# Rotary and plain halves of two attention heads handled as a pair in a two-layer hybrid encoder kernel

## What is computed

```python
q = (rms_norm(c_q, mla_q_norm_g[l]) @ mla_w_uq[l]).reshape(B, S, MLA_HEADS, MLA_QK)
kv = (rms_norm(c_kv, mla_kv_norm_g[l]) @ mla_w_ukv[l]).reshape(B, S, MLA_HEADS, MLA_NOPE + MLA_V)
k_nope, v_m = kv[..., :MLA_NOPE], kv[..., MLA_NOPE:]
k = jnp.concatenate([k_nope, jnp.broadcast_to(k_rope[:, :, None, :], ...)], axis=-1)
q, k = rms_norm(q, mla_qn_g[l]), rms_norm(k, mla_kn_g[l])
q = jnp.concatenate([q[..., :MLA_NOPE], rope(q[..., MLA_NOPE:], pos)], axis=-1)
k = jnp.concatenate([k[..., :MLA_NOPE], rope(k[..., MLA_NOPE:], pos)], axis=-1)
...
s = jnp.einsum('bqhd,bkhd->bhqk', q[:, q0:q1], k[:, :q1]).astype(jnp.float32) * scale
mask = (jnp.arange(q1) // CHUNK)[None, :] <= ((q0 + jnp.arange(Q_BLOCK)) // CHUNK)[:, None]
p = jax.nn.softmax(jnp.where(mask, s, -jnp.inf), axis=-1)
```

## Time and profile before

| | |
|---|---|
| profiled execution / its span | 1735.35 / 1733.6 us |
| median of the runs | 1735.27 us |
| PE busy | 1714.8 us, 8730 matmul records |
| DVE, ACT, POOL busy | 1104.6, 862.1, 296.0 us |
| granted TensorE clock | 0.999 of full speed |
| PE idle, named waits | 5.9 (first x), 4.3 (w_lo), 3.3 (L1518), 0.6 (L1442) us |

### The profile page before, as it was taken

One profiled execution on the slowest core, in us unless ns is written; L12 is line 12 of the kernel. 1 busy time (PEld: TensorE's weight loads), 2 busy tenths in 40 slices (PEclk: granted clock), 3 DMA queues, 4 the chain that ended last, 5 costly groups with the idle time before them and its releaser, 6 DMA issues.

```text
span 1733.6 us, 22527 instructions
## 1 busy us (share of the span) xinstructions
PE 1714.8 (99%) x8730; PEld 1435.9 (83%) x8730; DVE 1104.6 (64%) x1571; ACT 862.1 (50%) x1267; POOL 296.0 (17%) x440
## 2 busy tenths in 40 slices
PE   7999999999999999999999999999999999999998
PEld 6878888888888888888888788888888888888887
DVE  4667564656766647786656775755666666668853
ACT  6454543434455555555454445434445555655532
POOL 1011020210000025362410110110100000444500
PEclk9999999999999999999999999999999999999999
DMA  8866555655655556795687655656465555568764
GB/s 258 252 184 181 170 164 177 183 152 176 195 165 150 166 174 200 229 310 197 200 260 225 182 175 161 183 158 183 147 193 176 169 156 158 163 215 273 273 197 153
DMA packets 177475, 332.84 MB, mean 192 GB/s; under 512 B 20588, under 2 KB 33306, under 8 KB 177368
## 3 DMA queue, kind: packets, MB, share of 16 engines
q1 hardware_dynamic: 167784, 297.67, 56.0%
q0 software_dynamic: 9584, 33.73, 5.8%
HBM read 311.18 MB, written 16.78 MB: 189 GB/s over the span
## 4 chain that ended last, share of the span: by engine, by line
PE 93%; DVE 2%; ACT 1%; DMA 1%; POOL 1%; issue 1%; SPq 0%; DVEq 0%; ACTq 0%; POOLq 0%
PE D L652 82%; PE B L652 9%; DMA ring<-in_w_in 1%; DVE w_lo L1313 1%; POOL arena L591 1%; ACT w_hi L954 0%; DVE xy L1313 0%; ACT arena L954 0%; PE B L724 0%; PE B L826 0%; DVE arena L1436 0%; SPq L492 0%; PE B L708 0%; DMA xy<-in_x 0%; POOL arena L567 0%
## 5 line engine op out<-in xcount | busy, mean ns | idle before, releaser
L1313 DVE TENSOR_TENSOR w_lo<-ring,w_hi 128x1024 fp32r<-128x1024 f32 (+3 forms) x560 | 668.8, 1208 | 385.0 <-ACT w_hi L954 377.2
L954 ACT ACTIVATE w_hi<-ring 128x1024 fp32r<-128x1024 f32 (+3 forms) x560 | 572.6, 1037 | 373.5 <-PE D L652 272.9
L652 PE MATMUL D<-w_hi,ht_hi 128*128 128x512 f32 (+2 forms) x1728 | 689.0, 399 | 4.4 <-DVE w_lo L1313 4.3
L652 PE MATMUL D<-w_hi,ht_lo 128*128 128x512 f32 (+2 forms) x1728 | 667.4, 386 | 0.0
L652 PE MATMUL D<-w_lo,ht_hi 128*128 128x512 f32 (+2 forms) x1728 | 666.5, 386 | 0.0
L652 PEld LDWEIGHTS D<-w_hi,ht_hi 128*128 128x128 f32 x1728 | 326.0, 189 | 67.5 <-issue 5.9
L652 PEld LDWEIGHTS D<-w_hi,ht_lo 128*128 128x128 f32 x1728 | 325.1, 188 | 65.9
L652 PEld LDWEIGHTS D<-w_lo,ht_hi 128*128 128x128 f32 x1728 | 326.2, 189 | 57.9 <-issue 0.5
L954 ACT ACTIVATE arena<-B 64x128 f32<-64x128 f32 (+5 forms) x200 | 72.2, 368 | 246.3 <-PE B L652 212.6
L652 PEld LDWEIGHTS B<-arena 128*66 128x66 f32 (+4 forms) x1536 | 161.7, 164 | 32.4 <-issue 9.8
L591 POOL COPY arena<-arena 32x256 f32<-32x256 f32 x240 | 162.4, 676 | 126.9 <-DVE arena L1341 82.7
(11 more groups left out here) (155 smaller groups left out, 1288.7 us busy)
## 6 DMA issues: line engine op xcount, KB each, us to landing
ring<-in_w_in SPq DMA_DIRECT2D x368, 512.0 KB, 4.2
ring<-in_w_out SPq DMA_DIRECT2D x64, 512.0 KB, 5.0
ring<-in_w_br_mla SPq DMA_DIRECT2D x32, 512.0 KB, 5.2
gate_spill<-gev POOLq DMA_DIRECT2D x24, 512.0 KB, 4.8
arena<-gate_spill POOLq DMA_DIRECT2D x24, 512.0 KB, 6.0
ring<-in_mla_w_ukv SPq DMA_DIRECT2D x16, 512.0 KB, 4.1
...
```

The source lines that it names most:

```text
L652: return nc.tensor.matmul(o, a, b, start=start, stop=stop, skip_group_check=True)
L954: return nc.scalar.activation(o, i, fn, **kw)
L1313: return v.tensor_tensor(o, a, b, op)
```

## The change

For the two heads of a pair at once: PE transposes the plain parts into `B0` and `B1`, and the rotary parts of both heads together, as blocks of 128 columns, into `B2` (`QRH` and `KRH` hold two heads side by side). ACT copies `B0` and `B2`, DVE `B1`. The scores of head 0 go to `B3`, of head 1 to `B2`; their rotary part is a matmul over rows 0 to 63 for one head and over rows 64 to 127 for the other. DVE writes -1e30 into the masked quadrants in the banks with two memsets, takes four maxima; ACT takes four exponentials; the probabilities' transposes, copies (ACT head 0, DVE head 1) and value matmuls follow, and DVE scales with two operations. The gains are multiplied in with the scaling (`scalar_tensor_tensor`), so the two gain multiplications and the copy back before `ml_qk` go; the gain rows are loaded 192 wide. `ML_STEPS` has 7 entries that sum to 13.0 in place of 11 that sum to 15.4, which moves all positions, and the weights of pair 3 (`uq2`, `ukv2`) come after `sk`.

```diff
@@ -128,8 +123,8 @@
     g = [("wk", "w_in", C_KR, 256, KD)]
     g += wide("rr", C_RW) + wide("rk", C_RW + 512) + wide("rv", C_RW + 1024)
     g += gates[:1] + wide("cq", C_CQ) + wide("ckv", C_CKV)
-    g += gates[1:9] + pair(0) + pair(1) + gates[9:11] + wide("sq", C_SB) + pair(2)
-    g += wide("sk", C_SB + 512) + wide("sv", C_SB + 1024) + pair(3)
+    g += gates[1:9] + pair(0) + pair(1) + gates[9:11] + wide("sq", C_SB)
+    g += wide("sk", C_SB + 512) + pair(2) + wide("sv", C_SB + 1024) + pair(3)
     g += [("rg", "w_in", C_RG + 64, 448, KD)] + gates[11:]
     g += wide("mg0", C_MG) + wide("mg1", C_MG + 512) + wide("sg", C_SB + 1536)
...
@@ -159,7 +154,7 @@
 RW_STEPS = [1, 1.3, 1.2] + [0.9, 1] * LEVELS + [1] * 6
 LATENT_STEPS = [2, 2.5]
 GN_STEPS = [1] * 8
-ML_STEPS = [2.2, 2.2, 2.4] + [1, 1.3, 1, 1] * 2
+ML_STEPS = [2.4, 2.6, 1.6, 1.5, 2, 1.5, 1.4]
 SB_STEPS = [1.5, 3, 2, 2]
 RW_BEATS, GN_BEATS, ML_BEATS, SB_BEATS = len(RW_STEPS), len(GN_STEPS), len(ML_STEPS), len(SB_STEPS)
...
@@ -800,43 +795,54 @@
                     last.then_inc(lat_pe[l], 1)
                 beat()
 
-            def mla_head(m):
-
-                b, i = m // 2 % 2, m % 2
-                if i == 0:
-                    pe.wait_ge(ml_qk, 4 * l + m // 2 + 1)
-                if m:
-                    pe.wait_ge(ml_dve, 24 * l + 3 * m)
+            def mla_pair(p):
+
+                b = p % 2
+                pe.wait_ge(ml_qk, 4 * l + p + 1)
+                for i in range(2):
+                    for h in range(HALVES):
+                        nc.tensor.transpose(B[i][:, h * P:(h + 1) * P], MQ[:, b, h, i, 0:NOPE], ident)
+                        last = nc.tensor.transpose(B[i][:, 256 + h * P:256 + (h + 1) * P], MKV[:, b, h, i, 0:NOPE],
+                                                   ident)
+                    last.then_inc(ml_pe, 1)
+                for j, t in enumerate((QRH, KRH)):
+                    for h in range(HALVES):
+                        last = nc.tensor.transpose(B[2][:, j * 256 + h * P:j * 256 + (h + 1) * P],
+                                                   t[:, h, :, :].rearrange("p n c -> p (n c)"), ident)
+                last.then_inc(ml_pe, 1)
+                beat()
+                pe.wait_ge(ml_act, 16 * l + 4 * p + 1)
+                pe.wait_ge(ml_dve, 16 * l + 4 * p + 1)
+                own = [slice(64 * i, 64 * i + 64) for i in range(2)]
                 for h in range(HALVES):
-                    nc.tensor.transpose(B[0][:, h * P:(h + 1) * P], MQ[:, b, h, i, 0:NOPE], ident)
-                    nc.tensor.transpose(B[0][:, 256 + h * P:256 + (h + 1) * P], MKV[:, b, h, i, 0:NOPE], ident)
-                    nc.tensor.transpose(B[1][0:64, h * P:(h + 1) * P], MQ[:, b, h, i, NOPE:QK], ident)
-                    last = nc.tensor.transpose(B[1][0:64, 256 + h * P:256 + (h + 1) * P], KRH[:, h, i, :], ident)
+                    q, k, o = slice(h * P, (h + 1) * P), slice(256, 384 + h * P), slice(h * P, (2 * h + 1) * P)
+                    for i in range(2):
+                        mm(B[3 - i][:, o], QKN[:, i, q], QKN[:, i, k], True, False)
+                    for i in range(2):
+                        last = mm(B[3 - i][:, o], QKR[own[i], q], QKR[own[i], k], False, True)
                 last.then_inc(ml_pe, 1)
                 beat()
-                pe.wait_ge(ml_act, 24 * l + 3 * m + 1)
-                pe.wait_ge(ml_dve, 24 * l + 3 * m + 1)
-                mm(B[2][:, 0:128], QKN[:, 0:128], QKN[:, 256:384], True, False)
-                mm(B[2][:, 0:128], QKR[0:66, 0:128], QKR[0:66, 256:384], False, True)
-                mm(B[2][:, 128:384], QKN[:, 128:256], QKN[:, 256:512], True, False)
-                mm(B[2][:, 128:384], QKR[0:66, 128:256], QKR[0:66, 256:512], False, True).then_inc(ml_pe, 1)
-                beat()
-                pe.wait_ge(ml_act, 24 * l + 3 * m + 2)
-                for n in range(3):
-                    last = nc.tensor.transpose(B[3][:, n * P:(n + 1) * P], PP[:, n * P:(n + 1) * P], ident)
+                for i in range(2):
+                    pe.wait_ge(ml_act, 16 * l + 4 * p + 2 + i)
+                    for n in range(3):
+                        last = nc.tensor.transpose(B[i][:, n * P:(n + 1) * P], PP[:, i, n * P:(n + 1) * P], ident)
+                    last.then_inc(ml_pe, 1)
+                beat()
+                pe.wait_ge(ml_act, 16 * l + 4 * p + 4)
+                pe.wait_ge(ml_dve, 16 * l + 4 * p + 3)
+                for i in range(2):
...
-                    act.wait_ge(ml_dve, 24 * l + 3 * m + 2)
-                    f(PP[:, 0:128], B[2][:, 0:128], ACT.Exp, scale=ML_SCALE, bias=nb[:, 0:1], accum_out=den[:, 0:1])
-                    f(PP[:, 128:384], B[2][:, 128:384], ACT.Exp, scale=ML_SCALE, bias=nb[:, 1:2],
-                      accum_out=den[:, 1:2]).then_inc(ml_act, 1)
-                    beat()
-                    act.wait_ge(ml_pe, 32 * l + 4 * m + 3)
-                    f(PT, B[3][:, 0:384]).then_inc(ml_act, 1)
-                    beat()
-                    beat()
+                act.wait_ge(ml_pe, 28 * l + 7 * p + 1)
+                f(QKN[:, 0, :], B[0][:])
+                act.wait_ge(ml_pe, 28 * l + 7 * p + 3)
+                f(QKR, B[2][:]).then_inc(ml_act, 1)
+                beat()
+                act.wait_ge(ml_dve, 16 * l + 4 * p + 2)
+                for i in range(2):
+                    f(PP[:, i, 0:128], B[3 - i][:, 0:128], ACT.Exp, scale=ML_SCALE, bias=nb[:, i:i + 1],
+                      accum_out=den[:, i:i + 1])
+                    f(PP[:, i, 128:384], B[3 - i][:, 128:384], ACT.Exp, scale=ML_SCALE, bias=nb[:, 2 + i:3 + i],
+                      accum_out=den[:, 2 + i:3 + i]).then_inc(ml_act, 1)
+                beat()
+                act.wait_ge(ml_pe, 28 * l + 7 * p + 5)
+                f(PT[:, 0, :], B[0][:, 0:384]).then_inc(ml_act, 1)
+                beat()
+                beat()
 
...
                     for i in range(2):
                         k = 2 * h + i
-                        v.tensor_scalar(mq[:, h, i, :], mq[:, h, i, :], qss[:, k:k + 1], None, ALU.mult)
+                        v.scalar_tensor_tensor(mq[:, h, i, :], mq[:, h, i, :], qss[:, k:k + 1], GR[:, 0:QK],
+                                               ALU.mult, ALU.mult)
                         v.tensor_scalar(mk[:, h, i, 0:NOPE], mk[:, h, i, 0:NOPE], nss[:, k:k + 1], None, ALU.mult)
                         last = v.tensor_scalar(KRH[:, h, i, :], KR[:, h, :], nss[:, k:k + 1], None, ALU.mult)
                 link(last)
                 beat()
+                rope(mq[:, :, :, NOPE:QK], QRH, QS[:, 256:512], 2)
+                dve.sem_inc(ml_qk, 1)
+                beat()
+                dve.wait_ge(ml_pe, 28 * l + 7 * p + 2)
+                v.tensor_copy(QKN[:, 1, :], B[1][:]).then_inc(ml_dve, 1)
+                beat()
+                dve.wait_ge(ml_pe, 28 * l + 7 * p + 4)
+                for i in range(2):
+                    last = v.memset(B[3 - i][0:64, :].rearrange("p (n c) -> p n c", n=2)[:, :, 64:128], MASKED)
+                link(last)
+                for i in range(2):
+                    v.reduce_max(mx[:, i:i + 1], B[3 - i][:, 0:128], axis=X)
+                    last = v.reduce_max(mx[:, 2 + i:3 + i], B[3 - i][:, 128:384], axis=X)
+                link(last)
+                v.tensor_scalar(nb, mx, -ML_SCALE, None, ALU.mult).then_inc(ml_dve, 1)
+                beat()
+                dve.wait_ge(ml_act, 16 * l + 4 * p + 3)
+                link(v.reciprocal(rden, den))
+                dve.wait_ge(ml_pe, 28 * l + 7 * p + 6)
+                v.tensor_copy(PT[:, 1, :], B[1][:, 0:384]).then_inc(ml_dve, 1)
+                beat()
+                dve.wait_ge(ml_pe, 28 * l + 7 * p + 7)
                 for h in range(HALVES):
-                    last = tt(mq[:, h, :, NOPE:QK], mq[:, h, :, NOPE:QK],
-                              GR[:, 0:64].unsqueeze(1).to_broadcast([P, 2, 64]), ALU.mult)
-                link(last)
-                rope(mq[:, :, :, NOPE:QK], QS[:, 0:256].rearrange("p (h n c) -> p h n c", h=2, n=2), QS[:, 256:512], 2)
-                if p == 0:
-                    v.tensor_copy(QKR[64:66, :], con[64:66, K_MASK:K_MASK + 512])
-                v.tensor_copy(mq[:, :, :, NOPE:QK], QS[:, 0:256].rearrange("p (h n c) -> p h n c", h=2, n=2)
-                              ).then_inc(ml_qk, 1)
-                beat()
-                for m in (2 * p, 2 * p + 1):
-                    dve.wait_ge(ml_pe, 32 * l + 4 * m + 1)
-                    v.tensor_copy(QKR[0:64, :], B[1][0:64, :]).then_inc(ml_dve, 1)
-                    beat()
-                    dve.wait_ge(ml_pe, 32 * l + 4 * m + 2)
-                    v.reduce_max(mx[:, 0:1], B[2][:, 0:128], axis=X)
-                    link(v.reduce_max(mx[:, 1:2], B[2][:, 128:384], axis=X))
-                    v.tensor_scalar(nb, mx, -ML_SCALE, None, ALU.mult).then_inc(ml_dve, 1)
-                    beat()
-                    dve.wait_ge(ml_act, 24 * l + 3 * m + 2)
```

(66 more changed lines are left out.)

21 lines of the change are left out of this document (6 added, 15 removed).

## The result

The kernel after takes 1743.53 us (median of six runs, 1742.3 to 1744.64), the one before 1735.37 beside it: ratio 1.0045, 95% interval 1.0033 to 1.0057. It is slower, and outside the predicted range. The profiled execution took 1744.05 us.

A forecast was written before the change was run, and what follows sets the result against it. The prediction took PE's instruction stream as the bound (busy 1714.8 of 1733.6 us). Its terms, -3.5 + 0.6 + 3.8 - 0.9 = 0.0 us against 1735.35, gave a forecast of 1735.3 us, range 1729.4 to 1740.9.

The forecast's parts named there:

- Transposes (-3.5): On PE, a pair takes 12 transposes in place of 16, 0.44 us less each pair: -3.5 us in all.
- Rotary scores in halves (+0.6): In a pair's scores, half-height rotary matmuls run side by side, but state changes eat the gain: +0.6 us in all.
- the 0.37 for a change of state: At the rotary scores, going in and out of half-height tiling costs PE 0.37 us, twice a pair.
- The scan's wait for L1442: At the scan's last pair, PE's 0.44 us wait should go because earlier steps lengthen: -0.9 us in two layers.
- The probabilities' chain: From last score matmul to exponentials, DVE and ACT need 3.8 us a pair, in time for PE: 0.
- rival 4: PE waits 0.7 us at the probabilities' transposes in each of eight pairs: +5.6, 1740.9 us; chance 0.15.
- rivals 1 and 3: Rotary scores: either state changes come cheap, 1729.4 us, chance 0.20; or short halves don't overlap, 1740.6 us, chance 0.07.
- rival 2: No PE wait at the last pair: 1727.9 us at best, 1731.6 if half stays; chance 0.10.
- `rope` behind `rg`'s take-out: At the last pair, DVE's later rope makes PE's transposes wait at L804, once a layer: +3.8 us in all.
- So PE waits 3.7 us: At the last pair's transposes, PE arrives after 4.14 us but may begin at 7.9: a 3.7 us wait.
- Net +1.9 us a layer: At the last pair, the 3.7 us wait replaces the old 1.8 us wait at the scores: +3.8 us in all.
- I look for no other new wait in the scan: In the scan, whose steps all get 6% wider, no further new wait was expected; no size added.

The follow-up runs named there:

- experiment 7: The changed kernel with two ML_STEPS numbers changed, plus both token blocks' plain score matmuls ahead of both blocks' rotary ones: 1724.3 us, ratio 0.9931.
- experiment 8: The changed kernel with two ML_STEPS numbers changed, plus rotary matmuls over all 128 rows, none half-height: 1726.89 us, ratio 0.9945.
- experiment 1: The changed kernel with rope and ml_qk on DVE moved ahead of a pair's second beat, so ahead of rg's take-out: 1730.95 us, ratio 0.9975.
- Experiment 3: The changed kernel with POOL waiting for gate11 (chunk 192) ahead of its first row move: 1740.94 us, ratio 1.0032.
- Experiment 2: The changed kernel with four unused 512-column matmuls on PE ahead of the last pair's wait for ml_qk: 1739.57 us, ratio 1.0022.
- experiment 4: The kernel before, with rg's take-out on DVE ahead of gain, rope and copy in the last pair: 1751.55 us, ratio 1.0095.
- experiment 6: Experiment 1's kernel with POOL's second move behind the affine selects of the second stick-breaking pair: 1728.3 us, ratio 0.9955.

## Why the prediction was wrong

**Right.** Transposes (-3.5): 12 add 1.3 us. Rotary scores in halves (+0.6): 2.75 us against 2.7 forecast, and experiments 7 and 8 confirm the 0.37 for a change of state (0.39 in experiment 7, (0.66 + 0.13) / 2 = 0.40 in experiment 8). The scan's wait for L1442 went (-0.9). The probabilities' chain made no wait, so rival 4 fell; rivals 1 and 3 fell by the score stretch, rival 2 by the wait. The step that decided, `rope` behind `rg`'s take-out, was named with its place and releaser. Undoing that alone gave the 1730.95 us of experiment 1.

**Wrong, step by step.**
1. *"So PE waits 3.7 us"*: it waits 4.35. The term was mis-sized by `rope`: the 1.67 us came from a row in which POOL was idle, and it takes 2.19. The take-out of `rg` ends with the block transposes that release POOL's move, and in the new order `rope` stands right behind them; POOL's move slipped ahead of `gate11` by the same table. Experiment 3 gives 0.55 us of it back. +1.3 us.
2. *"Net +1.9 us a layer"*: a wait was priced as its length. Behind a wait of 4.35 us the array ran at 1.2 GHz, another 4.0 us in two layers. Experiment 2 removes just this, experiment 4 makes it in the old kernel. The page showed a full clock in all slices, but for a kernel whose waits there were 1.7 us; I took the level for a constant of the kernel. This is the largest step, and the sum had no term for it.
3. *"I look for no other new wait in the scan"*, and no term at all for the stick-breaking pairs: the table moves every position, and I walked through the latent pairs and the scan but not the stick-breaking pairs. The second begins at 199.5 instead of 200.0, which puts ACT's and DVE's work on chunk 200 behind the pair's first step and POOL's selects behind a late move. +2.6 us, experiment 6.

Once these three are taken out (experiment 6) the kernel takes 1728.3. The forecast's own terms without the wait give 1735.3 - 3.8 - 2 x 1.8 = 1727.9.

**Open.** 0.3 us of the difference to the median (0.8 to the profiled execution). Why the low stretch was 3.41 us long in one layer and 6.83 in the other was not settled; the mean granted clock of the six executions of after goes from 0.996 to 0.998, so its length seems to change from one execution to the next. Why POOL's second move takes 12.9 us in after and in experiment 1, and 11.0 in before and in experiment 6, was not followed up. Experiment 7's order with full-height rotary matmuls was not tried.
